# Results of the expert turns: product with a spread matrix, or rows written to DRAM and added once per layer

## The reference

```python
def moe_ffn(h, router_w, router_b, w1, w3, w2):
    t = h.reshape(-1, shape[-1])
    gates = route(t, router_w, router_b).astype(t.dtype)
    out = jnp.zeros_like(t)
    for e in range(N_EXPERTS):
        y = (jax.nn.silu(t @ w1[e]) * (t @ w3[e])) @ w2[e]
        out = out + gates[:, e:e + 1] * y
    return out.reshape(shape)
...
        x = x + g2 * moe_ffn(modulate(rms_norm(x, norm2_g[i]), sh2, sc2),
                             router_w, router_b, moe_w1[i], moe_w3[i], moe_w2[i])
```

## Time and profile before

| | us |
|---|---|
| median of 3 runs | 1036.12 (1034.21 to 1036.16) |
| the profiled execution, its own time | 1031.83 |
| its span, first to last instruction | 1030.0 |
| layer 0: expert turns | about 251 to 541 |
| layer 1: turns, then the wide turn | about 709 to 1020 |

### The profile page before, as it was taken

One profiled execution on the slowest core, in us unless ns is written; L12 is line 12 of the kernel. 1 busy time (PEld: TensorE's weight loads), 2 busy tenths in 40 slices (PEclk: granted clock), 3 DMA queues, 4 the chain that ended last, 5 costly groups with the idle time before them and its releaser, 6 DMA issues.

```text
span 1030.0 us, 16691 instructions
## 1 busy us (share of the span) xinstructions
PE 960.6 (93%) x5964; PEld 761.7 (74%) x5964; DVE 775.1 (75%) x956; ACT 616.8 (60%) x762; POOL 97.0 (9%) x160
## 2 busy tenths in 40 slices
PE   3899999998999999999996999888999999999996
PEld 0479884587787887887874986577787887888784
DVE  2544268556998988999977543667999989978994
ACT  3533315434878778778765422526778778757782
POOL 4092000001000000000000533010000000001000
PEclk8799999997999999999998999997999999999999
DMA  9997958747999999999995975839999999997971
GB/s 341 361 235 224 293 204 291 262 165 256 372 371 334 375 353 341 364 360 333 344 358 180 272 202 186 336 99 355 394 364 340 362 363 326 357 318 268 348 283 43
DMA packets 144737, 307.20 MB, mean 298 GB/s; under 512 B 13621, under 2 KB 44485, under 8 KB 144658
## 3 DMA queue, kind: packets, MB, share of 16 engines
q1 hardware_dynamic: 135360, 286.53, 78.9%
q0 software_dynamic: 7776, 18.96, 6.0%
q10 hardware_dynamic: 1530, 0.78, 0.3%
HBM read 296.54 MB, written 5.02 MB: 293 GB/s over the span
## 4 chain that ended last, share of the span: by engine, by line
PE 81%; DVE 10%; DMA 3%; issue 3%; ACT 2%; SPq 0%; ACTq 0%; DVEq 0%
PE ps L1713 16%; PE ps L1715 16%; PE ps L1714 16%; DVE wlo L1359 3%; PE ps L2223 3%; PE ps L1815 2%; PE ps L1725 2%; PE ps L1817 2%; PE ps L1816 2%; PE ps L1833 2%; PE ps L2248 2%; PE ps L2250 2%; PE ps L2249 2%; PE ps L1835 1%; PE ps L1834 1%
## 5 line engine op out<-in xcount | busy, mean ns | idle before, releaser
L1359 DVE TENSOR_TENSOR wlo<-raw,whi 128x1024 fp32r<-128x1024 f32 x384 | 454.2, 1219 | 32.4 <-ACT whi L747 31.2
L747 ACT CAST whi<-raw 128x1024 fp32r<-128x1024 f32 x384 | 396.9, 1052 | 113.5 <-PE ps L1715 101.0
L1713 PE MATMUL ps<-whi,xghi 128*128 128x512 f32 x480 | 192.4, 401 | 0.1
L1714 PE MATMUL ps<-whi,xglo 128*128 128x512 f32 x480 | 190.0, 396 | 0.0
L1715 PE MATMUL ps<-wlo,xghi 128*128 128x512 f32 x480 | 190.0, 396 | 0.0
L1088 DVE TENSOR_TENSOR wlo<-raw,whi 128x1024 fp32r<-128x1024 f32 x56 | 75.1, 1380 | 55.1 <-ACT whi L742 55.0
L1713 PE MATMUL ps<-whi,hidThi 128*128 128x512 f32 x256 | 102.5, 401 | 6.0 <-DVE hidTlo L1422 4.6
L1715 PEld LDWEIGHTS ps<-wlo,xghi 128*128 128x128 f32 x480 | 90.7, 189 | 21.5
L1713 PEld LDWEIGHTS ps<-whi,xghi 128*128 128x128 f32 x480 | 90.6, 189 | 21.4 <-DVE wlo L1359 0.6
L1714 PEld LDWEIGHTS ps<-whi,xglo 128*128 128x128 f32 x480 | 90.8, 189 | 20.4
L1715 PE MATMUL ps<-wlo,hidThi 128*128 128x512 f32 x256 | 101.7, 397 | 0.0
(11 more groups left out here) (321 smaller groups left out, 1486.1 us busy)
## 6 DMA issues: line engine op xcount, KB each, us to landing
raw<-in_moe_w SPq DMA_DIRECT2D x384, 512.0 KB, 5.4
raw<-in_w_mod SPq DMA_DIRECT2D x96, 512.0 KB, 6.0
raw<-in_na_w_in SPq DMA_DIRECT2D x24, 512.0 KB, 7.2
raw<-in_cf_pw_w SPq DMA_DIRECT2D x24, 512.0 KB, 8.8
mods<-mod_scratch POOLq DMA_DIRECT2D x9, 512.0 KB, 6.9
raw<-in_ab_w_out SPq DMA_DIRECT2D x8, 512.0 KB, 5.0
urep<-uT SPq DMA_DIRECT2D x64, 35.5 KB, 3.3
urep<-uT POOLq DMA_DIRECT2D x64, 35.5 KB, 3.2
```

The source lines that it names most:

```text
L747: A.copy(whi[:, (MOE_W[tn.L] + j) % SPL, :], raw[:, (MOE_U[tn.L] + j) % RAW, :]).then_inc(tn.sem("w_rounded"), 1)
L1359: V.tensor_tensor(wlo[:, n % SPL, :], raw[:, (MOE_U[L] + j) % RAW, :], whi[:, n % SPL, :], ALU.subtract).then_inc(tn.sem("unit_done"), 1)
L1713: T.matmul(dst, lhi, rhi, start=first, stop=False)
L1714: T.matmul(dst, llo, rhi, start=False, stop=False)
```

## The change

Results are no longer spread by products but by address. `yg` of a turn is written by an indirect DMA (`put_rows`) as 128 rows of 4 KB to the rows of its tokens in a DRAM scratch `y_scratch`; empty places go to a spare row, number 256. Before, the scratch is filled with zeros (so that tokens not written add nothing), and when all but the last turn's results are written, it is read back as `yback` (`rows_back`), and VectorE adds it to `x` with two 128x1024 additions, at unit 36 of the last turn (`BACK`). The last turn's own result still goes by products with `spread` (three results in layer 0 and two in layer 1 go by DRAM). `yg` may be overwritten when its put is complete (`y_free`). The token numbers are shifted by 256 in the constants and back on VectorE, so that empty places (product 0) become 256; `tok_scratch` gets a row 256 of zeros. The numbers are now also needed for tile 0. The turns' `y_round`, `y_remainder`, `scatter` and `x_add` go, also the first turn's with zeros.

```diff
             def tokens_out(L):
                 eng.wait_ge(h_set, 4 * L + 2)
-                eng.dma_start(tok_scratch[L].rearrange("(t p) d -> p t d", p=P), htok[:]).then_inc(tok_out[L], 16)
+                eng.dma_start(tok_scratch[L][0:SEQ].rearrange("(t p) d -> p t d", p=P), htok[:]).then_inc(tok_out[L], 16)
+                eng.wait_ge(y_clear, 2 * L + 1)
+                zeros = spread[:].bitcast(F32)
+                eng.dma_start(tok_scratch[L][SEQ].rearrange("(q n) -> q n", q=4), zeros[0:4, :]).then_inc(y_put, 16)
+                eng.wait_ge(y_put, 80 * L + 16)
+                eng.dma_start(y_scratch[L][0:SEQ].rearrange("(p t) (q n) -> p (t q) n", p=P, q=4),
+                              zeros.unsqueeze(1).broadcast_to([P, NT * D // SEQ, SEQ])).then_inc(y_put, 16)
                 eng.wait_ge(tok_out[L], 16)
...
+            def put_rows(L, tile):
+                eng.wait_ge(y_scaled, 6 * L + tile + 2)
+                eng.wait_ge(y_put, 80 * L + 32 + 16 * tile)
+                eng.indirect_dma_start(y_scratch[L], bass.IndirectOffsetOnAxis(ap=places[:, tile:tile + 1], axis=0), yg[:], None) \
+                   .then_inc(y_put, 16)
+
+            def rows_back(L):
+                eng.wait_ge(y_put, 80 * L + 32 + 16 * (LOOPS[L] - 1))
+                eng.dma_start(yback[:], y_scratch[L][0:SEQ].rearrange("(t p) d -> p t d", p=P)).then_inc(y_back, 16)
...
             for tile in range(1, GROUPS):
                 if tile > 1:
                     eng.wait_ge(gathered, tile)
-                fetch_rows(0, tile - 1)
+                fetch_rows(0, tile)
+                if tile > 1:
+                    put_rows(0, tile - 2)
+            put_rows(0, GROUPS - 2)
+            rows_back(0)
...
             for tile in range(1, GROUPS - 1):
                 eng.wait_ge(gathered, GROUPS + tile)
-                fetch_rows(1, tile - 1)
+                fetch_rows(1, tile)
+            for tile in range(LOOPS[1] - 1):
+                put_rows(1, tile)
+            rows_back(1)
...
@@ ScalarE, turn @@
-                        if j == 8 and looped:
-                            y_round(tn)
...
@@ VectorE @@
+                def y_free(g):
+                    eng.wait_ge(y_put, g * 16 + (80 * L + 16))
...
                 def y_scale(tn):
                     tn.wait(eng, "w_used", 0 if tn.spill is None else W_GROUP)
+                    if tn.spill is None:
+                        y_free(tn.g)
...
                             if j == 5:
                                 y_scale(tn)
-                            if j == 9:
-                                y_remainder(tn)
...
-                        if looped:
-                            for i in range(4):
-                                if j == SCATTER[i] + 6:
-                                    x_add(tn, i)
-                            if j == SCATTER[3] + 6:
...
+                        if looped and not ahead and j == BACK:
+                            at_ = tn.g + C_SLOT
+                            link(set_spread(cst[:, at_:at_ + 1]))
+                            eng.wait_ge(y_back, 16 * (L + 1))
+                            for t in range(NT):
+                                link(V.tensor_tensor(xres[:, t, :], xres[:, t, :], yback[:, t, :], ALU.add))
...
-                V.tensor_copy(places[:, 0:LOOPS[L] - 1], ps[:, BX, PLACES:PLACES + LOOPS[L] - 1]).then_inc(places_set, 1)
+                numbers = rt[:, T1, 0, 0:GROUPS]
+                link(V.tensor_scalar(numbers[:, 0:LOOPS[L]], ps[:, BX, PLACES:PLACES + LOOPS[L]], float(SEQ), None, ALU.add))
+                V.tensor_copy(places[:, 0:LOOPS[L]], numbers[:, 0:LOOPS[L]]).then_inc(places_set, 1)
...
@@ TensorE @@
-                for tile in range(1, LOOPS[L]):
+                for tile in range(LOOPS[L]):
                     for t in range(NT):
-                        ins = T.matmul(ps[:, BX, PLACES + tile - 1:PLACES + tile], pick[:, t, tile * P:(tile + 1) * P],
+                        ins = T.matmul(ps[:, BX, PLACES + tile:PLACES + tile + 1], pick[:, t, tile * P:(tile + 1) * P],
                                        token_number(t), start=(t == 0), stop=(t == NT - 1))
...
                         if prepare and j == WIDE_PREFIX:
-                            tn.wait(eng, "x_added", 4)
                             wide_prefix()
...
-                        if looped:
-                            for i in range(4):
-                                if j == SCATTER[i]:
-                                    scatter(tn, i)
...
+BACK = 36
...
-    k[:, C_TOK:C_TOK + NT] = np.arange(P)[:, None] + P * np.arange(NT)
+    k[:, C_TOK:C_TOK + NT] = np.arange(P)[:, None] + P * np.arange(NT) - SEQ
```

More of the change, by code:

```diff
@@ L177 @@
     "y_scaled": (lambda L: 1, lambda L: 6 * L),
[L178 to L181, removed]
+    "y_rounded": (lambda L: 0, lambda L: 2 * L),
+    "y_rest": (lambda L: 0, lambda L: 2 * L),
+    "scattered": (lambda L: 0, lambda L: 4 * L),
+    "x_added": (lambda L: 0, lambda L: 4 * L),
 }
@@ L185 @@
 HEAD = 2
-AFTER_LOOP = {"y_scaled": 10, "y_rounded": 10, "y_rest": 10, "scattered": 36, "x_added": 36, "gathered": 8, "xg_rounded": 16,
+AFTER_LOOP = {"y_scaled": 10, "y_rounded": 3, "y_rest": 3, "scattered": 8, "x_added": 8, "gathered": 8, "xg_rounded": 16,
               "xg_rest": 16, "picked": 0, "spread_T": 0, "spread_set": 0}
@@ L230, in program @@
             cf_pw1_w, cf_pw1_b, cf_dw_w, cf_dw_b, cf_ln_g, cf_ln_b, cf_pw2_w, cf_pw2_b, router_w, router_b,
-            moe_w1, moe_w3, moe_w2, final_g, consts, bias_scratch, mod_scratch, tok_scratch0, tok_scratch1, out):
+            moe_w1, moe_w3, moe_w2, final_g, consts, bias_scratch, mod_scratch, tok_scratch0, tok_scratch1, y_scratch0, y_scratch1, out):
     with ExitStack() as stack:
@@ L327, in program @@
         xrow = at("xrow", [P, D], 68)
+        yback = at("yback", [P, NT, D], 60)
         xg2hi = at("xg2hi", [P, KC, P], 60, F32R)
@@ L424, in program @@
         rows_of = sem("rows_of")
+        y_put = sem("y_put")
+        y_back = sem("y_back")
         xg_rounded = sem("xg_rounded")
@@ L686, in fetch_rows @@
                    .then_inc(rows_of, 16)
+            y_scratch = (y_scratch0, y_scratch1)
+            def put_rows(L, tile):
[6 more added lines that the diff above has]
+                eng.dma_start(yback[:], y_scratch[L][0:SEQ].rearrange("(t p) d -> p t d", p=P)).then_inc(y_back, 16)
             eng.wait_ge(h_set, 2)
@@ L1022, in _ @@
             table(ACT.Sqrt)
-            norm(3, [xres[:, 0], xres[:, 1]], [junk[:, 0], junk[:, 1]], lambda t: eng.wait_ge(x_added, 18 + 2 * t))
+            norm(3, [xres[:, 0], xres[:, 1]], [junk[:, 0], junk[:, 1]], lambda t: eng.wait_ge(x_added, 2 + 2 * t))
             round_second(2)
@@ L1521, in wide @@
                         V.tensor_copy(gate_of[:], ps[:, BX, GATES:GATES + PER_GROUP]).then_inc(tn.sem("spread_set"), 1)
-                        V.tensor_copy(places[:, 0:PER_GROUP - 1], ps[:, BX, GATES + PER_GROUP + 1:GATES + 2 * PER_GROUP]) \
-                         .then_inc(places_set, 1)
+                        y_free(GROUPS - 1)
+                        numbers = rt[:, T1, 0, 0:PER_GROUP - 1]
+                        link(V.tensor_scalar(numbers, ps[:, BX, GATES + PER_GROUP + 1:GATES + 2 * PER_GROUP], float(SEQ), None, ALU.add))
+                        V.tensor_copy(places[:, 0:PER_GROUP - 1], numbers).then_inc(places_set, 1)
                     for j in range(W_GROUP):
@@ L1579, in experts @@
                     turn(Turn(L, g, sems))
-                own[0] += LOOPS[L] - 1
                 turn(Turn(L, LOOPS[L] - 1, sems), ahead=0, prepare=L == 1)
@@ L1620, in _ @@
             eng.wait_ge(mod_in[7], 16)
-            eng.wait_ge(x_added, 18)
+            eng.wait_ge(x_added, 2)
             gained(fh, 0, mods[:, D:2 * D])
             mean_eps(8, 2)
-            eng.wait_ge(x_added, 20)
+            eng.wait_ge(x_added, 4)
             gained(fh, 1, mods[:, D:2 * D])
@@ L2385 @@
     for L in range(2):
-        args.append(nc.dram_tensor(f"tok_scratch{L}", [SEQ, D], F32, kind="Internal").ap())
+        args.append(nc.dram_tensor(f"tok_scratch{L}", [SEQ + 1, D], F32, kind="Internal").ap())
+    for L in range(2):
+        args.append(nc.dram_tensor(f"y_scratch{L}", [SEQ + 1, D], F32, kind="Internal").ap())
     args.append(nc.dram_tensor("out_0", [1, SEQ, D], F32, kind="ExternalOutput").ap())
```

1 line of the change is left out of this document (removed).

## The result

The changed kernel takes 1025.49 us (median of 4 runs, 1021.63 to 1026.68) against 1035.16 us for the kernel before on the same chip: ratio 0.9905, 95% interval 0.9885 to 0.9925, about 9.8 us less. Forecast were 13.1 us less and 1023.0; the time lies in the range. Five further runs of it gave 1024.03 us and 0.990 (0.9884 to 0.9917). The profiled execution took 1021.63 us, span 1019.8.

The account below looks back on a forecast made before the run. TensorE's in-order stream was taken to bound the turns. Matmuls -13.1, waits -2.2, one-column products +0.9, additions +0.3 and fill +1.0 sum to -13.1 us, from the median 1036.12 to 1023.0 us; range 1019.5 to 1031.

Parts of the forecast that it names:

- What bounds a turn: In steady expert turns TensorE's instruction order sets the end; about 4.4 us of delay to a load is absorbed.
- The matmuls: Seven turns each lose four pairs of scatter matmuls at 0.47 us a pair on TensorE: 13.1 us less.
- The two `x_add` waits: TensorE's waits at the second scatter of each layer's first turn go: 0.9 and 1.3 us, 2.2 us less.
- The one-column products: Two more per layer for tile 0's token numbers, before the first expert matmul: 0.9 us added (bounds 0.4 to 1.0).
- The additions at unit 36: VectorE's two adds of yback in each layer's last turn: 0.3 us charged in layer 1, nothing in layer 0.
- Puts and read-back: Transfers in the turns fit the DMA engines; in last turns 4.0 us of displaced loads against 4.4 slack: zero.
- A: Rival: scattered writes in the two last turns cost twice their bytes' time, gain only 5.9 us, 1030.2 us; chance 0.14.
- B: Rival: the 16 DMA engines bind once TensorE is faster, net +6.2 us, 1042.3 us; chance 0.07.
- C: Rival: layer 0's writes to row 256 queue up; excess above 4.4 us per put is paid five times; chance 0.07.
- D: Rival: fill and adds are free and VectorE's relief shortens stalls at turn ends, -15.9 us, 1020.2 us; chance 0.10.
- The zero fill in layer 1: Fill beside the first expert weights takes 3.7 us of engine time, stalling TensorE 1.0 us at unit 13 (bounds 0 and 2.2).

Follow-up runs that it names:

- narrow_scatter: The kernel before with the turns' scatter matmuls cut from 512 columns to 16, most of the turns' results lost: 1030.34 us, ratio 0.9953.
- no_dram: The changed kernel without fills, puts, read-back and additions of yback, dropping results of all but each layer's last turn: 1021.21 us, ratio 0.9866.
- fill_twice: The changed kernel with a second 1 MB zero fill behind the first in layer 1: 1024.38 us, ratio 0.9897; repeated as fill_twice_b: 1026.49 us, 0.9914.
- one_product: fill_early with the token number as a seventeenth column of the gates' product, so all one-column products go: 1017.19 us, ratio 0.9831.
- fill_early: The changed kernel with both layers' zero fills written at the start of layer 0, none in layer 1: 1019.71 us, ratio 0.9865.
- puts_twice: The changed kernel with every put also written into the other scratch, one after the other: 1024.49 us, ratio 0.9902.
- fill_four: The changed kernel with three more 1 MB fills, into spare rows, behind layer 1's fill: 1031.05 us, ratio 0.996.
- after_again: The changed kernel once more, unchanged: 1024.03 us, ratio 0.990 to the kernel before.

## Why the prediction was right, and where it was short

**What bounds a turn: right.** narrow_scatter took only columns from TensorE and got 1.04 us per middle turn for the 1.0 worked out, with VectorE at its full 67 us.

**The matmuls, 13.1 us: right to about 1 us.** 1.88 us per turn were forecast (seven of them are 13.2, which the sum had as 13.1); the middle turns gave 1.74 each, layer 1's second 1.87, the third 1.7 (with the additions, for which 0.3 was charged). In no_dram and fill_twice the middle turn gave 1.87 and 1.98, and fill_twice has its puts, so the 0.1 us that is missing is within what these turns move by.

**The two `x_add` waits, 2.2 us: gone as forecast, in layer 0 for a little less.** The first turns lost both in the changed kernel. With the fill out of the way, layer 1's entry and first turn is 90.54 us; forecast without the fill was 93.22 - 1.88 - 1.3 + 0.44 = 90.5. narrow_scatter shows that this relief is VectorE's part: without it the matmuls taken out of the first turns are worth nothing. In layer 0 the stretch fell at equal clock by 1.8 us on average, for 2.3 forecast (91.18, 91.74, 90.71, 91.93, 91.19 and 90.59 us against 92.96 and 93.14), with 1.3 us between the shortest and the longest.

**The one-column products, 0.9 us: right in price.** Twelve records at 0.11 us became sixteen (1.33 to 1.77 us in the chain); one_product, which takes them all out, gained in time what they cost (3.3 us in the chain, 3.5 by the ratios), though its profile shows only part of it in layer 1.

**The additions at unit 36: right.** The timeline of VectorE shows them without a wait ahead, directly behind `set_spread`, and the next unit at once behind them; TensorE lists no wait for a remainder there. The whole turn fell by 1.68 us, 0.2 less than the 1.88 of the matmuls, for 0.3 charged.

```profile
896.15 0.34 DVE L1438 TENSOR_SCALAR spread<-posB,cst 128x256 fp32r<-128x256 f32 x1
896.53 2.48 DVE L1504 TENSOR_TENSOR xres<-xres,yback 128x1024 f32<-128x1024 f32 x2
899.05 2.36 DVE L1386 TENSOR_TENSOR wlo<-raw,whi 128x1024 fp32r<-128x1024 f32 x2
```

**Puts and read-back, nothing: right.** no_dram equals fill_early, and puts_twice equals the changed kernel. Rivals A (scattered writes beyond the slack), B (the engines are the bound) and C (the writes to the spare row queue up) fall for the turns with puts: a put lands in 7.0 us, a fetch in 6.1, and twice the puts cost nothing. At the start of layer 1's first turn, where there are no puts, the loads do set the pace (next part). D (more than forecast) falls with its free fill. The Trainium skill's 358 GB/s (DMA: Bandwidth & Descriptors, "Where 436 GB/s comes from") does not bind here: a 71 us window over the second turn of layer 1 shows 374 GB/s.

**The zero fill in layer 1: the step that failed.** The mechanism was forecast, its size was not: charged were 1.0 us (bounds 0 and 2.2), measured 3.0 to 3.9 us in the profiled stretch (93.52 and 94.39 against 90.54) and 3.6 us in time. I set the fill's engine time (3.7 us, above the 2.5 us per fill that fill_four gives in time) against the lead of one unit, number 13, and let 2.7 us of it be absorbed. The place was wrong, and the lead was not there.

TensorE found units late from the third on, in several places, but the wait that counts is the last one, and that is at unit 9 (the tenth, counting six expert matmuls a unit). What leads to it, in the changed kernel: ScalarE gets the load of unit 8 and casts it, loads a table, computes the first `silu`, and only then casts unit 9; VectorE forms its remainder, and TensorE goes on.

```profile
713.65 1.05 ACT L777 CAST whi<-raw 128x1024 fp32r<-128x1024 f32 x1 [0.30 <-DMA raw<-in_moe_w]
714.72 1.28 ACT L925 ACT_TABLE_LOAD   x1
716.01 0.60 ACT L925 ACTIVATE silu<-ps 128x512 f32<-128x512 f32 x1
...
718.86 0.50 PE L1745 MATMUL ps<-whi,xghi 128*128 128x512 f32 x1 [1.13 <-DVE wlo L1386]
```

The same in the profiles with and without fills, in us after the entry's `htok`:

| profile | fills beside the first weights | ScalarE casts unit 8 | TensorE starts unit 9 | from there to the fourth `hidThi` |
|---|---|---|---|---|
| fill_early | 0 | 33.48 | 39.34, no wait | 51.20 |
| no_dram | 0 | 34.08 | 39.29, waited 0.95 | 51.07 |
| changed | 1 | 37.26 | 42.47, waited 1.13 | 51.05 |
| puts_twice | 1 | 37.46 | 42.67, waited 1.14 | 51.05 |
| after_again | 1 | 37.97 | 43.18, waited 1.01 | 51.21 |
| fill_twice | 2 | 40.11 | 45.32, waited 1.10 | 51.21 |
| fill_twice_b | 2 | 40.97 | 46.18, no wait listed (0.3 late) | 51.06 |
| fill_four | 4 | 45.94 | 51.15, waited 1.14 | 51.06 |

Wherever a fill stands beside the first weights, TensorE starts unit 9 5.21 us after the cast of unit 8, and from there the way is always 51.1 to 51.2 us long. So the stretch is as long as this one load is late: (45.94 - 33.78) / 4 = 3.0 us per fill, with 33.78 the mean of the two without one, and nothing of it is absorbed. Without a fill there is no lead either, since no_dram waits at unit 9 and fill_early comes to it at the same moment. This also says why less time at the lower clock did not make no_dram shorter (10.2 us of it, 90.36 us long, for 13.6 and 90.54).

The windows fit this: in the kernel before the loads come at 384 to 406 GB/s from 720 to 745 us and only then slacken; in the changed kernel, whose layer 1 begins 6.9 us sooner, they still come at full rate there. Two windows of each, before and then changed (last columns: granted clock, DMA share, GB/s):

```profile
740.00:745.00 5.00, 5.00 (x25) 4.08 (x24) 5.00 (x7) 3.56 (x5) 0.00 (x0) 1.00 1.03 406
745.00:750.00 5.00, 5.00 (x23) 4.07 (x22) 4.58 (x5) 4.33 (x5) 0.00 (x0) 1.00 0.93 317
```

```profile
740.00:745.00 5.00, 5.00 (x23) 4.04 (x22) 5.00 (x5) 4.47 (x6) 0.00 (x0) 1.00 1.03 392
745.00:750.00 5.00, 5.00 (x23) 4.06 (x22) 4.82 (x6) 3.79 (x5) 0.00 (x0) 1.00 1.05 387
```

And the fill came earlier against the loads than worked out, 0.7 us after the first issue, so it stood beside all of the first nine loads. The Trainium skill's rule that each DMA engine takes turns between the queues it has work for (DMA: Bandwidth & Descriptors, "Queues, rings and completion order") goes with what the traces show: loads issued on SyncE's queue land later as soon as a fill is under way on POOL's queue, unit 8 by 3.0 us for each 1 MB.

That accounts for 2.0 of the 3 us that are missing (0.3 us more in that stretch, where 1.7 less was forecast). The rest, about 1 us, is 0.1 us in each middle turn and 0.5 us in layer 0's first, both no larger than what repeats differ by; it stays unassigned. What a second fill costs behind a first is 2.1 to 3.7 us in the profiles; why the times show only 0 to 1.5 us stays open.

## What to carry to other kernels

Price a matmul in a full stream by the distance to the next one, and read the waits before believing a busy share: DMA engines that were 0.98 busy took on 4% more traffic (370 for 355 GB/s) at no cost, since their queue was waiting for slots. A transfer is free only where the loads have a lead; right after a stage opens, when every load is consumed as it lands, each megabyte costs its engine time (3.0 us here, none of it hidden), so write scratch zeros a stage earlier. To price such a delay, find the last wait of the stretch, not the first or the sum. And where two engines are late together, relief has to come to both: in the first turns shortening TensorE alone (narrow_scatter) gave -0.2 and +0.3 us, for 1.04 in a middle turn.

## What the runs showed of the hardware

An indirect write of 128 rows of 4 KB from SBUF to DRAM landed in 6.6 to 7.7 us beside full-rate weight loads in the changed kernel, though part of its rows (of layer 0's 512 places 256 are empty) went to one address; its issue took POOL 1.36 to 1.74 us, that of a fetch 0.94 to 1.04 us in seven of eight cases and 1.71 in one.

A fill on another queue also slowed the issuing of the weight loads: each of the first ten of layer 1 took SyncE 0.37 to 0.41 us to issue in the kernel before and up to 0.62 in fill_early, but up to 1.8 us in the changed kernel and, of nine, up to 4.0 us in fill_four.

The time at TensorE's lower clock in one and the same stretch of the program moved between profiles, from 6.8 to 20.5 us between the layers, and the stretch went roughly with it, from 147.2 to 150.9 us. Only the turns at full clock in all profiles repeat, to 0.05 us in the two profiles of the kernel before and to 0.25 us over all versions with puts. With two profiles a difference of 1 to 2 us in a stretch with gaps in TensorE's work says nothing; only the repeat of the kernel before showed that.
